# The last tile of a decoder step's second down product, computed in two token parts

## The chip, the cores and the metric

One NeuronCore of a Trainium2 chip runs the whole program. The metric is the device time of one execution in microseconds, as the median of several. Beside it stands one execution taken by the hardware profiler, from which all rows below come.

## What is computed

One inference step of a one-layer decoder. 528 prompt tokens (16 learned meta tokens and 512 of the prompt) and 32 sample tokens (8 sequences of 4) pass through the same weights, D = 1024, feed-forward width 2816, everything in float32:

```python
x = x + 0.5 * swiglu(rmsnorm(x, ffn1_norm), ...)
h = rmsnorm(x, mix_norm)          # mLSTM branch and differential attention, gates, output projection
x = x + merged @ w_out
x = x + 0.5 * swiglu(rmsnorm(x, ffn2_norm), ffn2_w_gate, ffn2_w_up, ffn2_w_down)
y_prompt = rmsnorm(xp[:, N_META:], final_norm)
y_sample = rmsnorm(xs, final_norm)
# rmsnorm(x, g): x * rsqrt(mean(x*x over the 1024 channels) + EPS) * g
```

The meta tokens are dropped from `y_prompt`. New keys, values and states are outputs too; they are stored in the middle of the program and the change does not touch them.

## The kernel before

Activations lie channel by partition: `X` is 128 x 8 x 560, eight tiles (`DT`) of 128 channels, and the 560 columns (`T`) are the tokens: 16 meta, 512 prompt, 32 sample. The second feed-forward block leaves the meta tokens out (`c0 = NMETA`), so its products run over 544 tokens, as two halves of 272.

**Products.** Each float32 product is three float32r matmuls: high part of the weights times high and low part of the activations, and low part of the weights times the high part (L391 to L405). `down2` has eight output tiles (L810 to L814). One tile takes two weight panels, s = 0 and 1, of 11 blocks each (`KD`), in the buffers `raw[s]`, `w_hi[s]`, `w_lo[s]`. SyncE loads a panel (L365), ScalarE makes its high part (L370), VectorE its low part (L374). Per panel the order is half, block, term: 66 matmuls of 272 columns, so 132 for a tile. Even tiles go to PSUM banks 0 and 1, odd ones to 2 and 3.

**After each down2 tile i.** VectorE multiplies the PSUM by `rh` (half the reciprocal root of the second norm, L1925) and adds it to `X` (L1927). ScalarE writes `xg`, X times the final gain (L1859), and `sq`, the squares of X (L1860, L1464). VectorE adds the squares to the running sum `acc` (L1901). TensorE transposes `xg` one tile late (`back_y(i-1)`, L825 to L833) in five pieces of 112 tokens into banks 4 to 7, and VectorE copies them to `ytok` (L2477), whose rows are tokens: row tile t holds tokens 112 t to 112 t + 111, meta tokens included.

**After the last tile (i = 7).** `down_last` (L835 to L846) lets TensorE transpose tile 6, then tile 7, then sum `acc` over the channels by five products of a 128 x 112 piece with a column of ones, into bank 4. ScalarE makes the reciprocal root of the mean, `r5`, by Ln (L1864) and Exp (L1866). ScalarE scales row tiles 1 and 3 (L1870), VectorE 0, 2 and 4 (L2489). SyncE stores each row tile when it is scaled, in the order of t, row tile 4 in two pieces (prompt, sample), six stores in all (L766 to L774), and waits for all stores (L775).

What sets the order: every engine has its instruction stream written out by hand, and semaphores are waited on by count. `mm_done[s]` says a panel's product is done, `evac[e]` a bank pair is free, `x_ready` X is updated, `sq_ready` squares are there, `acc_done` the running sum, `xg_ready`, `yt_full`, `yt_done` the gain copy, its transposes, its row copy; `y5_full`, `y5_log`, `y5_ready` the steps of the root; `y_act`, `y_dve` scaled row tiles.

Of the kernel before, what the change touches and what calls it, by code (L numbers as in the profile page):

```python
# [20 lines left out]
D = 1024  # L21
SEQ, NMETA, NB, DSEQ = 512, 16, 8, 4
# [9 lines left out]
T = NP_ + NS  # L32
H2 = T // 2
DT = D // 128
FT = DFF // 128
KD = FT // 2
# [12 lines left out]
G_FFN1, G_MIX, G_FFN2, G_FINAL, G_CW, G_CB, G_ML, G_SUB, G_N = 0, 8, 16, 24, 32, 64, 72, 80, 81  # L49
# [9 lines left out]
C_EPS = C_M1 + 1  # L59
# [58 lines left out]
def build(nc, ins, outs, const_ap):  # L118
    f32, f32r, i32 = mybir.dt.float32, mybir.dt.float32r, mybir.dt.int32
    ACT = mybir.ActivationFunctionType  # L120
    ALU = mybir.AluOpType
# [5 lines left out]
    with ctx:  # L127
# [31 lines left out]
        h_hi = at("h_hi", [128, FT, T], f32r, R)  # L159
        h_lo = at("h_lo", [128, FT, T], f32r, R + FT * T * 4)  # L160

        xtok = at("xtok", [112, 5, D], f32, R)
        ytok = at("ytok", [112, 5, D], f32, xn0)
        xg = at("xg", [128, 2, T], f32, xn0 + 5 * D * 4)
        vecs = at("vecs", [G_N, 128], f32, R + 5 * D * 4)
        lrow = at("lrow", [1, 4, DHD], f32, R + 5 * D * 4 + 512)
# [15 lines left out]
        small2 = at("small2", [128, 448], f32, RW + 5 * T * 4)  # L182
# [82 lines left out]
        ps = ctx.enter_context(nc.psum_tensor("ps", [128, 8, 512], f32))  # L265
# [15 lines left out]
        wlast = wrow.rearrange("p (b t) -> p b t", t=DSEQ)[:, :, DSEQ - 1]  # L281
        wbc = small2[:, 80:208].rearrange("p (h s) -> p h s", h=HM)
        dec8 = small2[0:NB, 208:212]
        r5 = small2[0:112, 400:405]
        r0 = small2[0:112, 408:418]
        srm = small2[:, 320:336].rearrange("p (b k m) -> p b k m", b=2, k=4)
        SAs = small2[:, 336:400].rearrange("p (b m c) -> p b m c", b=2, m=2)
# [215 lines left out]
        def wide(bank, rows_, cols):  # L503

            return ps[0:rows_, bank:bank + 2, :].rearrange("p b n -> p (b n)")[:, 0:cols]
# [79 lines left out]
                 8: ((0, (4,)), (1, (0, 1)), (0, (5,)), (1, (2, 3)), (0, (6, 7)), (1, (4, 5)))}  # L585
        IDLE = {0: 12, 2: 4, 4: 5}
        HI0 = (0, DT, 3 * DT + 1)
        GAIN = (G_FFN1, G_MIX, G_FFN2, G_FINAL)
        block = ctx.enter_context(nc.Block())

# [2 lines left out]
        def _(sp):  # L593
# [169 lines left out]
            stream(p_wo)  # L763
            stream(up2)
            stream(down2)
            for t in (0, 1, 2, 3, 4):  # L766
                sp.wait_ge(y_act if t % 2 else y_dve, t // 2 + 1)
                if t == 0:
                    sp.dma_start(y_prompt[0, 0:96, :], ytok[16:112, 0, :]).then_inc(stored, 16)
                elif t < 4:  # L770
                    sp.dma_start(y_prompt[0, 112 * t - 16:112 * t + 96, :], ytok[:, t, :]).then_inc(stored, 16)
                else:
                    sp.dma_start(y_prompt[0, 432:512, :], ytok[0:80, 4, :]).then_inc(stored, 16)
                    sp.dma_start(y_sample.rearrange("b t d -> (b t) d"), ytok[80:112, 4, :]).then_inc(stored, 16)  # L774
            sp.wait_ge(stored, 16 * (5 + 6 + 6))  # L775


        @block.tensor
        def _(pe):
            def transpose(out, in_, k):  # L780
                return pe.transpose(out, in_, con[0:k, C_ID:C_ID + k])  # L781
# [28 lines left out]
            def down_tile(p, u, j, e, tiles=None):  # L810
                at_ = None if tiles is None else lambda k: u.lo0 + k + 1
                pe.wait_ge(evac[e], j + p.ev0)
                product(pe, p, j * 2 + e, 0, 2 * e, h_hi, h_lo, 0, True, False, tiles=tiles, tile_at=at_)
                product(pe, p, j * 2 + e, 1, 2 * e, h_hi, h_lo, KD, False, True, tiles=tiles, tile_at=at_)  # L814

            def down(p, u):
# [5 lines left out]
                        down_tile(p, u, j, e)  # L822
                loop(pe, p, body, 2, first=1)

            def back_y(i):  # L825

                pe.wait_ge(xg_ready, i + 1)
                if i >= 2:
                    pe.wait_ge(yt_done, i - 1)
                for t in range(5):  # L830
                    mm = transpose(ps[0:112, 4 + 2 * (i % 2) + t // 4, 128 * (t % 4):128 * (t % 4) + 128],
                                   xg[:, i % 2, 112 * t:112 * t + 112], 128)
                mm.then_inc(yt_full, 1)  # L833

            def down_last(p, u):  # L835
                for j in range(p.n // 2):
                    for e in range(2):
                        down_tile(p, u, j, e, tiles=tile_lo if j == 0 and e == 0 else None)
                        if 2 * j + e >= 1:
                            back_y(2 * j + e - 1)  # L840
                back_y(DT - 1)
                pe.wait_ge(acc_done, 3 * (DT - 1))
                pe.wait_ge(yt_done, DT - 1)
                for t in range(5):
                    mm = pe.matmul(ps[0:112, 4, t:t + 1], acc[:, 112 * t:112 * t + 112], ones[:, 0:1], start=True, stop=True)
                mm.then_inc(y5_full, 1)  # L846

            def pair(p, xs_, first=0):
                def body(j, _q, _jn):
# [602 lines left out]
        def _(act):  # L1452
            def copy(out, in_, scale=1.0):
                return act.activation(out, in_, ACT.Copy, scale=scale)
# [396 lines left out]
            rms(2, up2)  # L1851
            gated(up2, ACT.Silu, h_hi)

            def last_tile(i):

                act.wait_ge(x_ready, DT + i + 1)
                if i >= 2:
                    act.wait_ge(yt_full, i - 1)
                copy(xg[:, i % 2, :], X[:, i, :], scale=gcol[:, G_FINAL + i:G_FINAL + i + 1]).then_inc(xg_ready, 1)  # L1859
                square(3, i)  # L1860

            down(down2, last_tile)
            act.wait_ge(y5_full, 1)
            act.activation(r5, ps[0:112, 4, 0:5], ACT.Ln, bias=con[0:112, C_EPS:C_EPS + 1], scale=1.0 / D).then_inc(y5_log, 1)  # L1864
            act.wait_ge(y5_log, 1)
            act.activation(r5, r5, ACT.Exp, scale=-0.5).then_inc(y5_ready, 1)  # L1866
            act.wait_ge(yt_done, DT)
            act.wait_ge(y5_ready, 1)
            for t in (1, 3):
                copy(ytok[:, t, :], ytok[:, t, :], scale=r5[:, t:t + 1]).then_inc(y_act, 1)  # L1870


        @block.vector
        def _(v):
# [46 lines left out]
            def down(p, r, each):  # L1921
                def add(j, e):
                    i = 2 * j + e
                    v.wait_ge(mm_done[1], i + p.before + 1)
                    v.tensor_tensor(tok(t2[e], p), two(2 * e, p), tok(rh, p), ALU.mult).then_inc(evac[e], 1)  # L1925
                    v.wait_ge(evac[e], j + p.ev0 + 1)
                    v.tensor_tensor(X[:, i, p.c0:], X[:, i, p.c0:], t2[e][:, p.c0:], ALU.add).then_inc(x_ready, 1)  # L1927
                    each(i)

                for j in range(p.n // 2):  # L1930
                    for s in range(2):
                        split_lo(v, p, j * 2 + 1, s)
                    add(j, 0)
                    if j < p.n // 2 - 1:
                        for s in range(2):
                            split_lo(v, p, j * 2 + 2, s)
                        add(j, 1)
                    else:
                        prepare(p.next, 0, 0)
                        add(j, 1)  # L1940
                        prepare(p.next, 0, 1)
# [533 lines left out]
            def rows_y(i):  # L2475
                v.wait_ge(yt_full, i + 1)
                v.tensor_copy(ytok[:, :, 128 * i:128 * i + 128],  # L2477
                              wide(4 + 2 * (i % 2), 112, 640).rearrange("p (t n) -> p t n", n=128)).then_inc(yt_done, 1)

            def last_tile(i):  # L2480
                squares(3, i)
                if i >= 1:
                    rows_y(i - 1)
            down(down2, 3, last_tile)
            rows_y(DT - 1)
            v.wait_ge(yt_done, DT)
            v.wait_ge(y5_ready, 1)
            for t in (0, 2, 4):
                v.tensor_scalar(ytok[:, t, :], ytok[:, t, :], r5[:, t:t + 1], None, ALU.mult).then_inc(y_dve, 1)  # L2489


        @block.gpsimd
# [36 lines left out]
```

## Time and profile before

| | us |
|---|---|
| median of 3 executions | 1712.9 (1712.69 to 1718.42) |
| the profiled execution | 1710.33 |
| its span, first to last instruction | 1708.5 |
| TensorE busy in the span | 1655.7 (97%) |
| VectorE, ScalarE busy | 765.4 (45%), 554.6 (32%) |
| chain that ended last: TensorE, ScalarE, VectorE, DMA | 88%, 3%, 3%, 3% |
| last product of down2 ends | at 1689.53 |
| first store of y issued | at 1698.43 |

The span is shorter than the time by 1.8 us, which lie outside the first and last instruction. Starts are microseconds from the span's start. Matmuls are pipelined, so a single matmul's duration is longer than its distance to the next; the pace of a stream is read from starts, or from a chain's stretch divided by its count. "Granted clock" is the share of TensorE's full clock that the chip allowed, 1.0 for 2.4 GHz and 0.5 for 1.2 GHz.

### The profile page before, as it was taken

What the parts mean: (1) busy time and instruction counts of PE and PEld (TensorE: products, weight loads), DVE (VectorE), ACT (ScalarE), POOL (GpSimd) and SP (SyncE); (2) the same over time, 40 slices, a digit from 0 to 9 for tenths busy, and PEclk for the clock granted to TensorE, in tenths of its full rate; (3) what the DMA queues carried; (4) which work ended last, traced back from release to release, by engine and by line L of the source; (5) the groups of instructions that cost most, each with busy time, mean ns of one, the idle gap of its engine ahead of it and who ended that gap; (6) DMA issues with size and microseconds to landing.
All of it is one profiled execution on the core that took longest, in us unless ns stands there. A gap on an engine that the chain in (4) does not pass through costs nothing.

```text
span 1708.5 us, 30634 instructions
## 1 busy us (share of the span) xinstructions
PE 1655.7 (97%) x12836; PEld 1568.2 (92%) x12836; DVE 765.4 (45%) x1150; ACT 554.6 (32%) x845; POOL 4.2 (0%) x20
## 2 busy tenths in 40 slices
PE   7999999999999889999999999989999999999996
PEld 7999999999988667999999977679999999999996
DVE  4333333333682443553337678664453333333332
ACT  5222222222333432542111257562233222222222
POOL 0000000000000000000000000000000000000000
PEclk9999999999999999999999999999999999999998
DMA  5222223222322740233333240643322222223221
GB/s 139 77 86 86 86 86 98 88 85 76 77 75 56 242 153 1 74 87 86 100 92 98 72 183 26 203 145 97 86 87 87 86 86 86 86 86 102 86 85 53
DMA packets 253836, 161.77 MB, mean 95 GB/s; under 512 B 8234, under 2 KB 246047, under 8 KB 253762
## 3 DMA queue, kind: packets, MB, share of 16 engines
q1 hardware_dynamic: 253616, 160.67, 32.3%
q8 instruction: 55, 0.90, 0.2%
q14 instruction: 19, 0.16, 0.0%
q10 hardware_dynamic: 146, 0.04, 0.0%
HBM read 143.14 MB, written 16.40 MB: 93 GB/s over the span
## 4 chain that ended last, share of the span: by engine, by line
PE 88%; ACT 3%; DVE 3%; DMA 3%; issue 1%; SPq 1%; ACTq 0%; DVEq 0%
PE ps L402 73%; PE ps L781 2%; PE ps L969 2%; PE ps L933 1%; PE ps L1257 1%; PE ps L1185 1%; PE ps L1128 1%; PE ps L1301 1%; PE ps L1018 1%; DMA Cb<-in_state_C 1%; DVE small L2329 1%; PE ps L1113 1%; PE ps L1182 1%; PE ps L1260 1%; DMA raw<-in_w_in 0%
## 5 line engine op out<-in xcount | busy, mean ns | idle before, releaser
L402 PE MATMUL ps<-xn_hi,w_hi 128*128 128x272 f32 (+1 forms) x2192 | 635.7, 290 | 5.6 <-DVE w_lo L374 3.4
L402 PE MATMUL ps<-xn_hi,w_lo 128*128 128x272 f32 (+1 forms) x2192 | 637.5, 291 | 0.0
L402 PE MATMUL ps<-xn_lo,w_hi 128*128 128x272 f32 (+1 forms) x2192 | 634.5, 289 | 0.0
L370 ACT ACTIVATE w_hi<-raw 128x1024 fp32r<-128x1024 f32 (+1 forms) x200 | 222.2, 1111 | 823.4 <-PE ps L402 819.6
L402 PEld LDWEIGHTS ps<-xn_hi,w_hi 128*128 128x128 f32 x2192 | 413.6, 189 | 7.2 <-DVE w_lo L374 4.0
L402 PEld LDWEIGHTS ps<-xn_hi,w_lo 128*128 128x128 f32 x2192 | 413.5, 189 | 0.0
L402 PEld LDWEIGHTS ps<-xn_lo,w_hi 128*128 128x128 f32 x2192 | 412.5, 188 | 0.0
L374 DVE TENSOR_TENSOR w_lo<-raw,w_hi 128x1024 fp32r<-128x1024 f32 (+1 forms) x200 | 257.6, 1288 | 214.0 <-ACT w_hi L370 213.6
L402 PE MATMUL ps<-h_lo,w_hi 128*128 128x280 f32 (+1 forms) x704 | 204.7, 291 | 0.0
L402 PE MATMUL ps<-h_hi,w_hi 128*128 128x280 f32 (+1 forms) x704 | 204.7, 291 | 0.0
L402 PE MATMUL ps<-h_hi,w_lo 128*128 128x280 f32 (+1 forms) x704 | 204.6, 291 | 0.0
L402 PEld LDWEIGHTS ps<-h_lo,w_hi 128*128 128x128 f32 x704 | 132.7, 189 | 0.0
L402 PEld LDWEIGHTS ps<-h_hi,w_lo 128*128 128x128 f32 x704 | 132.7, 188 | 0.0
L402 PEld LDWEIGHTS ps<-h_hi,w_hi 128*128 128x128 f32 x704 | 132.6, 188 | 0.0
L1914 DVE TENSOR_TENSOR tB<-ps,tA 128x560 f32<-128x560 f32 (+1 forms) x44 | 32.3, 733 | 160.9 <-PE ps L402 160.9
L1909 DVE TENSOR_TENSOR tA<-ps,rn 128x560 f32<-128x560 f32 (+1 forms) x44 | 32.2, 733 | 132.5 <-PE ps L402 132.5
L1491 ACT ACTIVATE tA<-tA 128x544 f32<-128x544 f32 (+1 forms) x60 | 38.8, 646 | 0.0
L402 PE MATMUL ps<-m_hi,w_hi 128*128 128x272 f32 x128 | 36.9, 288 | 0.8 <-DVE m_lo L2458 0.8
L402 PE MATMUL ps<-o_hi,w_hi 128*128 128x272 f32 x128 | 37.1, 290 | 0.0
L402 PE MATMUL ps<-o_hi,w_lo 128*128 128x272 f32 x128 | 37.0, 289 | 0.0
L402 PE MATMUL ps<-hm_hi,w_lo 128*128 128x272 f32 x128 | 37.0, 289 | 0.0
L402 PE MATMUL ps<-o_lo,w_hi 128*128 128x272 f32 x128 | 36.9, 288 | 0.0
(372 smaller groups left out, 2026.8 us busy)
## 6 DMA issues: line engine op xcount, KB each, us to landing
raw<-in_w_in SPq DMA_DIRECT2D x56, 512.0 KB, 3.8
raw<-in_ffn_w_gate SPq DMA_DIRECT2D x44, 512.0 KB, 3.8
raw<-in_ffn_w_up SPq DMA_DIRECT2D x44, 512.0 KB, 3.8
raw<-in_ffn_w_down SPq DMA_DIRECT2D x32, 704.0 KB, 4.5
Cb<-in_state_C SPq DMA_DIRECT2D x32, 256.0 KB, 4.1
out<-Cb SPq DMA_DIRECT2D x32, 256.0 KB, 3.0
pages<-in_cache_k SPq DMA_DIRECT2D x16, 512.0 KB, 4.7
pages<-in_cache_v SPq DMA_DIRECT2D x16, 512.0 KB, 4.9
```

The costliest lines, as they stand in the source:

```text
L370: act.activation(w_hi[s][:, 0:p.nk, :], raw[s][:, 0:p.nk, :], ACT.Copy).then_inc(hi_done[s], 1)
L374: v.tensor_tensor(w_lo[s][:, 0:p.nk, :], raw[s][:, 0:p.nk, :], w_hi[s][:, 0:p.nk, :].bitcast(f32), ALU.subtract).then_inc(lo_done[s], 1)
L402: mm = pe.matmul(ps[:, bank + half, 0:p.half], w[s][:, k, :], x[:, k0 + k, cols], start=first and k == 0 and a == 0, stop=last and k == p. ...
L781: return pe.transpose(out, in_, con[0:k, C_ID:C_ID + k])
L933: mm = pe.matmul(ps[0:(128, 128, 128, 128, TAIL, 128)[blk], ring_bank(n) + h // 2, DHM * (h % 2):DHM * (h % 2) + DHM], x, mlw[:, 0, i, :], ...
L969: mm = pe.matmul(ps[:, ring_bank(n) + half, 0:H2], mlw[:, 1 if kind == "k" else 2, 2 * h + k, 128 * m:128 * m + 128], cc[:, 2 * h + k, hal ...
L1018: mm = pe.matmul(ps[:, 6, DHM:2 * DHM], vtok[:, blk, DHM * h + 128 * vt:DHM * h + 128 * vt + 128], ktok[:, blk, DHM * h:DHM * h + DHM], st ...
L1113: mm = pe.matmul(ps[:, half, 0:H2], con[0:HM, C_SEL + 128 * h:C_SEL + 128 * h + 128], rows[:, row, half * H2:(half + 1) * H2], start=True, ...
L1128: mm = pe.matmul(out, km[:, 2 * h + k, t0:t0 + nt], qm[:, 2 * h + k, q0:q0 + nq], start=k == 0, stop=k == 1)
L1491: act.activation(tA[:, p.c0:], tA[:, p.c0:], func).then_inc(evac[0], 1)
L1909: v.tensor_tensor(tok(tA, p), two(0, p), tok(rn, p), ALU.mult).then_inc(g_in, 1)
L1914: v.tensor_tensor(tok(tB, p), two(2, p), tok(tA, p), ALU.mult).then_inc(evac[1], 1)
```

## The change

The last tile of `down2` is computed in two parts of tokens, both panels each: part 0 has tokens 16 to 271 (256 columns, bank 2), part 1 tokens 272 to 559 (288 columns, bank 3). Row tiles now have 128 tokens and start behind the meta tokens (`YROWS`: 16, 144, 272, 400, and 432 for the last, which overlaps tile 3 and of which only the 32 sample rows are used). Part 0 has row tiles 0 and 1, part 1 has 2, 3 and 4.

TensorE: `back_y(6)` comes between the parts. In part 1, after its 21st matmul (s = 0, k = 6), comes part 0's block `last_rows(0)`: column sums into bank 0, of `acc` (up to tile 6) and of tile 7's squares, accumulated by TensorE, then two transposes. `last_rows(1)` follows the last product. ScalarE and VectorE have a part 0 and a part 1 of evacuation, add, squares (now ahead of the gain copy), Ln, Exp and row scaling; tile 7's squares are no longer added to `acc` by VectorE. ScalarE has one more Ln of a single element between its parts. Stores: row tiles 0, 1, 2 and the sample rows by SyncE, row tile 3 by ScalarE's queue. Five stores of 512, 512, 512, 512 and 128 KB.

```diff
+        YROWS = [NMETA + 128 * t for t in range(4)] + [T - 128]
+        LAST = ((NMETA, 256, (0, 1)), (NMETA + 256, 288, (2, 3, 4)))
...
-            for t in (0, 1, 2, 3, 4):
-                sp.wait_ge(y_act if t % 2 else y_dve, t // 2 + 1)
...
+            for t, ready in ((0, (y_dve, 1)), (1, (y_act, 1)), (2, (y_dve, 2))):
+                sp.wait_ge(*ready)
+                sp.dma_start(y_prompt[0, 128 * t:128 * t + 128, :], ytok[:, t, :]).then_inc(stored, 16)
+            sp.wait_ge(y_dve, 3)
+            sp.dma_start(y_sample.rearrange("b t d -> (b t) d"), ytok[96:128, 4, :]).then_inc(stored, 16)
...
+            def last_rows(part):
+
+                pe.wait_ge(acc_done, 3 * (DT - 1) - 1)
+                pe.wait_ge(evac[0], down2.ev0 + DT // 2)
+                pe.wait_ge(sq_ready, 3 * DT + part)
+                for t in LAST[part][2]:
+                    for i, squares in enumerate((acc, sq)):
+                        mm = pe.matmul(ps[:, 0, t:t + 1], squares[:, YROWS[t]:YROWS[t] + 128], ones[:, 0:1],
+                                       start=i == 0, stop=i == 1)
+                mm.then_inc(y5_full, 1)
+                pe.wait_ge(xg_ready, DT + part)
+                pe.wait_ge(yt_done, DT - 2)
+                back_rows(DT - 1, LAST[part][2])
+
+            def last_down(p):
+
+                pe.wait_ge(evac[1], p.ev0 + DT // 2 - 1)
+                for part, (c0, n, _) in enumerate(LAST):
+                    for s in range(2):
+                        pe.wait_ge(lo_done[s], p.before + DT)
+                        for k in range(KD):
+                            for a, (w, x) in enumerate(((w_hi, h_hi), (w_hi, h_lo), (w_lo, h_hi))):
+                                mm = pe.matmul(ps[:, 2 + part, 0:n], w[s][:, k, :], x[:, s * KD + k, c0:c0 + n],
+                                               start=s == 0 and k == 0 and a == 0,
+                                               stop=s == 1 and k == KD - 1 and a == 2)
+                            if part == 1 and s == 0 and k == 6:
+                                last_rows(0)
+                    mm.then_inc(mm_done[part], 1)
+                    if part == 0:
+                        back_y(DT - 2)
+                last_rows(1)
...
-                back_y(DT - 1)
-                pe.wait_ge(acc_done, 3 * (DT - 1))
-                pe.wait_ge(yt_done, DT - 1)
-                for t in range(5):
-                    mm = pe.matmul(ps[0:112, 4, t:t + 1], acc[:, 112 * t:112 * t + 112], ones[:, 0:1], start=True, stop=True)
...
+            def last_part(part):
+
+                c0, n, rows_ = LAST[part]
+                cols, r = slice(c0, c0 + n), slice(rows_[0], rows_[-1] + 1)
+                act.wait_ge(x_ready, 2 * DT + part)
+                act.wait_ge(acc_done, 3 * (DT - 1) - 1)
+                act.activation(sq[:, cols], X[:, DT - 1, cols], ACT.Square).then_inc(sq_ready, 1)
+                act.wait_ge(yt_full, DT - 2)
+                scaled(DT - 1, cols)
+                act.wait_ge(y5_full, part + 1)
+                act.activation(r5[:, r], ps[:, 0, r], ACT.Ln, bias=con[:, C_EPS:C_EPS + 1], scale=1.0 / D).then_inc(y5_log, 1)
+                act.wait_ge(y5_log, part + 1)
+                act.activation(r5[:, r], r5[:, r], ACT.Exp, scale=-0.5).then_inc(y5_ready, 1)
+                act.wait_ge(y5_ready, part + 1)
+                act.wait_ge(yt_done, DT + part)
+                t = rows_[1]
+                copy(ytok[:, t, :], ytok[:, t, :], scale=r5[:, t:t + 1]).then_inc(y_act, 1)
...
+                if i == DT - 1:
+                    last_part(0)
+                    act.activation(small[0:1, 60:61], con[0:1, 0:1], ACT.Ln)
+                    last_part(1)
+                    act.wait_ge(y_act, 2)
+                    act.dma_start(y_prompt[0, 384:512, :], ytok[:, 3, :]).then_inc(stored, 16)
+                    return
...
+            def last_parts():
+
+                for part, (c0, n, rows_) in enumerate(LAST):
+                    o, x = tB[:, c0:c0 + n], X[:, DT - 1, c0:c0 + n]
+                    v.wait_ge(mm_done[part], down2.before + DT)
+                    v.tensor_tensor(o, ps[:, 2 + part, 0:n], rh[:, c0:c0 + n], ALU.mult).then_inc(evac[1], 1)
+                    v.wait_ge(evac[1], down2.ev0 + DT // 2 + part)
+                    v.tensor_tensor(x, x, o, ALU.add).then_inc(x_ready, 1)
+                    if part == 0:
+                        rows_y(DT - 2)
+                    t0, nt = rows_[0], len(rows_)
+                    v.wait_ge(yt_full, DT + part)
+                    v.tensor_copy(ytok[:, t0:t0 + nt, 128 * (DT - 1):D],
+                                  wide(6, 128, 640)[:, 128 * t0:128 * (t0 + nt)].rearrange("p (t n) -> p t n", n=128)
+                                  ).then_inc(yt_done, 1)
+                    v.wait_ge(y5_ready, part + 1)
+                    v.wait_ge(yt_done, DT + part)
+                    v.tensor_scalar(ytok[:, t0, :], ytok[:, t0, :], r5[:, t0:t0 + 1], None, ALU.mult).then_inc(y_dve, 1)
+                v.tensor_scalar(ytok[96:128, 4, :], ytok[96:128, 4, :], r5[96:128, 4:5], None, ALU.mult).then_inc(y_dve, 1)
```

## Rows read from the trace of the kernel before

**Rows 1.** The page's head and its first part: busy us, share, instructions.
```profile
span 1708.5 us, 30634 instructions
PE 1655.7 (97%) x12836; PEld 1568.2 (92%) x12836; DVE 765.4 (45%) x1150; ACT 554.6 (32%) x845; POOL 4.2 (0%) x20
```

**Rows 2.** The chain that ended last, its end: start, us, what.
```profile
1672.33 0.55 PE ps L781 x5
1672.88 16.65 PE ps L402 x132
...
1689.55 0.74 DVE tB L1925
...
1690.31 0.74 DVE X L1927
...
1691.07 0.76 ACT xg L1454
1691.83 0.57 ACT sq L1464
...
1692.42 0.74 DVE acc L1901
1693.16 0.75 DVE ytok L2477
...
1694.05 1.69 PE ps L845 x10
...
1695.76 0.27 ACT small L1864
...
1696.04 1.28 ACT L1866
...
1697.34 0.22 ACT small L1866
...
1697.64 1.15 ACT ytok L1454
```

**Rows 3.** Timeline of VectorE in the first down product (280 columns): start, us.
```profile
369.46 0.73 DVE L1925 TENSOR_TENSOR tB<-ps,rh 128x560 f32<-128x560 f32 x1
...
386.51 0.73 DVE L1925 TENSOR_TENSOR tA<-ps,rh 128x560 f32<-128x560 f32 x1
```

**Rows 4.** Timeline of TensorE, narrow float32 passes and 128-column transposes.
```profile
1083.99 0.42 PEld L781 LDWEIGHTS ps<-con,pages 128*128 128x128 f32 x4 [0.60 <-ACT KT L1454]
...
1085.35 1.16 PE L1361 MATMUL ps<-small,Psm 128*128 128x16 f32 x11
```

**Rows 5.** Groups by form: count, busy us, mean ns.
```profile
L2015 DVE TENSOR_TENSOR E<-ps,rn 128x280 f32<-128x280 f32 x8 | 3.5, 441 | 0.0
...
L1828 ACT ACTIVATE ofac<-qkv 128x256 f32<-128x256 f32 x1 | 0.4, 404 | 0.0
```

**Rows 6.** VectorE's timeline of tile 6, and windows behind the products (PEclk).
```profile
1678.26 0.74 DVE L1901 TENSOR_TENSOR acc<-acc,sq 128x560 f32<-128x560 f32 x1 [1.39 <-ACT sq L1464]
...
1694.00:1694.45 0.45, 0.41 (x4) 0.44 (x5) 0.45 (x1) 0.00 (x0) 0.00 (x0) 0.95 0.00 0
1694.45:1695.00 0.55, 0.55 (x5) 0.55 (x5) 0.18 (x1) 0.00 (x0) 0.00 (x0) 0.50 0.00 0
```

**Rows 7.** Timeline of SyncE's queue: start, us.
```profile
1002.02 5.27 SPq L737 DMA_DIRECT2D out<-vtok  x6
...
1658.44 0.37 SPq L365 DMA_DIRECT2D raw<-in_ffn_w_down  x1
1698.43 0.36 SPq L769 DMA_DIRECT2D out<-ytok  x1
1698.85 3.24 SPq L771 DMA_DIRECT2D out<-ytok  x3
```

**Rows 8.** Windows over stores (last: DMA share, GB/s); an issue's KB, us to landing.
```profile
1003.50:1007.50 4.00, 3.26 (x28) 1.21 (x18) 3.77 (x11) 2.08 (x8) 0.00 (x0) 1.00 1.01 413
1699.50:1705.50 6.00, 0.00 (x0) 0.00 (x0) 0.23 (x1) 0.33 (x1) 0.00 (x0) 0.50 0.99 296
...
out<-kout SPq DMA_DIRECT2D x4, 512.0 KB, 2.6
```

More of the change, by code:

```diff
@@ L162, in build @@
         xtok = at("xtok", [112, 5, D], f32, R)
-        ytok = at("ytok", [112, 5, D], f32, xn0)
+        ytok = at("ytok", [128, 5, D], f32, xn0)
         xg = at("xg", [128, 2, T], f32, xn0 + 5 * D * 4)
@@ L283, in build @@
         dec8 = small2[0:NB, 208:212]
-        r5 = small2[0:112, 400:405]
+        r5 = small2[:, 400:405]
         r0 = small2[0:112, 408:418]
@@ L765, in _ @@
             stream(down2)
-            for t in (0, 1, 2, 3, 4):
-                sp.wait_ge(y_act if t % 2 else y_dve, t // 2 + 1)
[L768 to L775, printed above, removed]
+            for t, ready in ((0, (y_dve, 1)), (1, (y_act, 1)), (2, (y_dve, 2))):
[3 more added lines that the diff above has]
+            sp.dma_start(y_sample.rearrange("b t d -> (b t) d"), ytok[96:128, 4, :]).then_inc(stored, 16)
+            sp.wait_ge(stored, 16 * (5 + 6 + 5))
         @block.tensor
@@ L823, in down, with back_rows @@
                 loop(pe, p, body, 2, first=1)
+            def back_rows(i, rows_):
+                for t in rows_:
+                    mm = transpose(ps[:, 4 + 2 * (i % 2) + t // 4, 128 * (t % 4):128 * (t % 4) + 128],
+                                   xg[:, i % 2, YROWS[t]:YROWS[t] + 128], 128)
+                mm.then_inc(yt_full, 1)
             def back_y(i):
@@ L829, in back_y @@
                     pe.wait_ge(yt_done, i - 1)
-                for t in range(5):
-                    mm = transpose(ps[0:112, 4 + 2 * (i % 2) + t // 4, 128 * (t % 4):128 * (t % 4) + 128],
-                                   xg[:, i % 2, 112 * t:112 * t + 112], 128)
-                mm.then_inc(yt_full, 1)
-            def down_last(p, u):
[L836 to L840, printed above, removed]
-                back_y(DT - 1)
-                pe.wait_ge(acc_done, 3 * (DT - 1))
-                pe.wait_ge(yt_done, DT - 1)
-                for t in range(5):
-                    mm = pe.matmul(ps[0:112, 4, t:t + 1], acc[:, 112 * t:112 * t + 112], ones[:, 0:1], start=True, stop=True)
-                mm.then_inc(y5_full, 1)
+                back_rows(i, range(5))
@@ L848, in pair @@
+            def down_last(p, u):
+                for i in range(DT - 1):
+                    down_tile(p, u, i // 2, i % 2, tiles=tile_lo if i == 0 else None)
+                    if i >= 1:
+                        back_y(i - 1)
+                last_down(p)
             def pair(p, xs_, first=0):
@@ L1852, in _, with scaled @@
             gated(up2, ACT.Silu, h_hi)
-            def last_tile(i):
+            def scaled(i, cols):
+                copy(xg[:, i % 2, cols], X[:, i, cols], scale=gcol[:, G_FINAL + i:G_FINAL + i + 1]).then_inc(xg_ready, 1)
+            def last_part(part):
[14 more added lines that the diff above has]
+                copy(ytok[:, t, :], ytok[:, t, :], scale=r5[:, t:t + 1]).then_inc(y_act, 1)
+            def last_tile(i):
+                if i == DT - 1:
[5 more added lines that the diff above has]
+                    return
                 act.wait_ge(x_ready, DT + i + 1)
@@ L1858, in last_tile @@
                     act.wait_ge(yt_full, i - 1)
-                copy(xg[:, i % 2, :], X[:, i, :], scale=gcol[:, G_FINAL + i:G_FINAL + i + 1]).then_inc(xg_ready, 1)
+                scaled(i, slice(0, T))
                 square(3, i)
             down(down2, last_tile)
[L1863 to L1870, printed above, removed]
         @block.vector
@@ L1937, in down @@
                         add(j, 1)
+                    elif p is down2:
+                        last_parts()
                     else:
@@ L2477, in rows_y @@
                 v.tensor_copy(ytok[:, :, 128 * i:128 * i + 128],
-                              wide(4 + 2 * (i % 2), 112, 640).rearrange("p (t n) -> p t n", n=128)).then_inc(yt_done, 1)
+                              wide(4 + 2 * (i % 2), 128, 640).rearrange("p (t n) -> p t n", n=128)).then_inc(yt_done, 1)
             def last_tile(i):
@@ L2483, in last_tile @@
                     rows_y(i - 1)
-            down(down2, 3, last_tile)
[L2485 to L2489, printed above, removed]
+            def last_parts():
[16 more added lines that the diff above has]
+                v.tensor_scalar(ytok[96:128, 4, :], ytok[96:128, 4, :], r5[96:128, 4:5], None, ALU.mult).then_inc(y_dve, 1)
+            down(down2, 3, last_tile)
         @block.gpsimd
```

## The prediction

> **What bounds the kernel now.** I read the page's first part first: TensorE is busy 97% of the span [rows 1], so between the ends of the program only TensorE's own stream counts. The change touches the last 36 us, so I read the chain of waits there [rows 2]. It has three stretches. Tile 7's products run as one unbroken row of 132 matmuls from 1672.88 to 1689.53. Then a serial tail crosses the engines: evacuation, residual add, gain copy, square, running sum, copy of tile 6's rows, column sums, Ln, a table load, Exp. The first row scale starts at 1697.64, so rstd is there at about 1697.6, 8.1 us after the products. The third stretch is stores: the first is issued at 1698.43 [rows 7] and the span ends at 1708.5, 10.1 us later, with the DMA engines full for most of it [rows 8]. So 19.0 us lie behind the last product, over half of it data movement that could have begun earlier.
>
> **The products.** Splitting 2 x 272 tokens into 256 and 288 keeps the number of matmuls (132) and the number of columns (544 per k and term). Pitch now: 16.65 / 132 = 126.1 ns at 272 columns [rows 2]. In the first down product tiles follow at 386.51 - 369.46 = 17.05 us, 129.2 ns at 280 columns [rows 3]. That is 0.39 ns per column, so I take 119.9 ns for 256 and 132.3 ns for 288; 66 of each give 16.65 us again. If a 256-column matmul went no faster than a 272-column one, this would cost 66 x 6.2 = 0.4 us. Part 0 then ends at 1672.88 + 7.91 = 1680.8.
>
> **What is inserted into the product row.** First, tile 6's five transposes now stand ahead of part 1, where before they hid under the evacuation. No row costs them at exactly this place; five cost 0.55 us in the chain [rows 2], and a 128-column transpose costs 0.42 / 4 = 105 ns [rows 4], so 0.6 us. Second, after 21 matmuls of part 1 (1680.8 + 0.6 + 21 x 0.132 = 1684.2) TensorE does part 0's sums and rows: two row tiles x two sources (the running sum and tile 7's squares) x two passes = 8 passes, then two transposes. The nearest warm row with a full stationary matrix and a narrow moving one is 11 passes in 1.16 us; less the last one's length (0.25) that is 91 ns a pass [rows 4]. The cold one is 10 passes in 1.69 us [rows 2], 169 ns. So 0.7 to 1.35 us for the sums and 0.2 for the transposes; with the edges I take 1.1 us, warm because products stand on both sides (bounds 0.9 and 1.6). The last product therefore ends at 1689.53 + 0.6 + 1.1 = 1691.2.
>
> **Do the inserted waits hold it?** VectorE evacuates and adds part 0 in 0.42 us each (441 ns at 280 columns [rows 5]); ScalarE squares 256 columns in 0.40 us [rows 5]. Squares are there at about 1682.1 and the gain copy at 1682.6, while TensorE asks at 1684.2: 2.1 us of slack, and behind this wait stand 45 products. The running sum it also asks for, up to tile 6, was made at 1678.26 + 0.74 [rows 6]. The rest of part 0 runs beside those 45 products (5.95 us): Ln 0.27, load 1.28, Exp 0.22, scaling a row tile 1.15 on ScalarE, then the added Ln with its load, 1.5. ScalarE is free at about 1685.1 + 1.85 + 1.15 + 1.5 = 1689.6; it is wanted at 1692.1, when part 1's residual is added. VectorE's share (copy of tile 6's rows 0.8, part 0's rows 0.45, one scale 0.78) ends near 1687.7, before 1691.2. Without that cover each would cost its own length; the smallest margin is ScalarE's 2.5 us. Part 0's two stores, 1.05 MB, are issued near 1688 and need 2.5 to 3.5 us [rows 8], so they are gone before the last ones start. Nothing else waits in SP's queue: its last weight load was issued at 1658.44 [rows 7].
>
> The trace has both table loads as 1.28 us, Exp's following Ln at once [rows 2]. The Trainium skill (ScalarE: Activation LUTs, What ACT_TABLE_LOAD costs) charges a switch 2.66 us, because a drain of 1.38 us is added. No row of this tail shows that drain. With it on part 0's two remaining loads ScalarE would be free at 1692.4, 0.3 us late.
>
> **The tail after the last product.** Evacuation and add at 288 columns: 0.44 + 0.44 and two handoffs of 0.02 = 0.92 us, where 1.52 us stood. The square, now ahead of the gain copy: 0.43 (between 0.40 at 256 and 0.66 at 560) + 0.02 = 0.45. The gain copy (0.76), the running sum (0.74), the row copy (0.75) leave the path. The sums now have 12 passes in place of 10, because the squares are added by TensorE: 12 x 91 ns + 0.2 = 1.3 us warm, 2.2 us cold. The granted clock fell from 1.0 to 0.5 (2.4 to 1.2 GHz) at about 1694.4, 4.9 us after the products ended [rows 6]; the new sums run from 1.4 to 2.7 us behind them, so I take them as warm. Ln, load, Exp with handoffs as now: 1.83. Sum: 0.02 + 0.92 + 0.45 + 1.3 + 1.83 = 4.5 us, where 8.1 stood. The added Ln only repeats what holds today, where Ln's load also runs under TensorE's work; Exp's load stays on the path. Transposes and row copy of part 1 lie under Ln and Exp. rstd is there at 1691.2 + 4.5 = 1695.7, 1.9 us earlier than now. The scale of 1024 columns up to the issue stays 0.8 us: first late store at 1696.6.
>
> **The stores.** Now six of 2.23 MB in total follow that point; then three of 1.18 MB (512, 512 and 128 KB). Rows of the DMA engines: 2.23 MB of 112-row tiles moved at 296 GB/s while the engines were 99% busy, yet the 512 KB stores of 128 rows of values (`vtok`, issued from 1002.0 on [rows 7]) moved at 413 GB/s, equally busy, and one such store alone lands 2.6 us after its issue [rows 8]. The new stores have the shape of the latter. Around the movement lie 0.6 us ahead of it and 1.6 us behind it (10.07 less 2.23 MB at about 282 GB/s over all of it, 7.9 us). New tail: 0.6 + 1.18 / 0.413 = 2.85 + 1.6 = 5.05 us; at 282 GB/s it is 6.4. The ScalarE store is ready 0.35 us and the sample rows 0.8 us behind the first, both inside its 1.3 us of movement, so neither adds. I take the fast rate, since shape and size match. The Trainium skill (DMA: Bandwidth & Descriptors, The descriptor swizzle) says that with 128 partitions each DMA engine writes one port's partitions; this trace's 413 against 296 GB/s agrees in direction.
>
> **Sum.** Span: 1696.6 + 5.05 = 1701.7, 6.8 us less than 1708.5. The profiled execution took 1710.33 us, 1.8 outside its span, so 1703.5 us. The median shown, 1712.9, is 2.6 above the profiled one; I carry that over: **1706.1 us**, 0.4% less.
>
> **Rivals.**
> *Forecast, stores at 413 GB/s, everything inserted hidden but 1.7 us*: gain 6.8. Chance 0.55.
> *The rate stays at 282 to 296 GB/s*, because the late state of the chip and not the row count sets it: tail 6.4, gain 5.4. For it: the 112-row stores are the only ones at the end of the program, with the other engines idle. Against: equal busy share at unequal bytes. Chance 0.2.
> *Sums and inserted block at cold prices* (169 ns a pass): 0.5 + 0.9 more, gain 5.4, and 3.6 with a 256-column floor as well; with slow stores too 2.2. For it: narrow matmuls are the only work there. Against: the granted clock was full 4.9 us on. Chance 0.13.
> *A larger gain*: Exp's load falls off the path, 1.28 more: 8.1 us. The Trainium skill (ScalarE: Activation LUTs, Table sets) names a set with both ln and exp. Against: this trace reloads between them, and so will the same two calls. Chance 0.08.
> *Slower than before*: TensorE stands in the block inside part 1, with 45 products behind it. Each us costs a us, so it decides from 6.8 us of standing; if it stands so long that the clock falls, as 4.9 us after the products in [rows 6], the 45 products take 169 / 91 of their time, 5.95 x 0.86 = 5.1 more, and the total is 4.9 + 5.1 - 6.8 = 3.2 us slower, 1716.1. It needs part 0's chain to take 7 us instead of the 1.8 worked out. Chance 0.04.
> The change does what it says: the stores of part 0 wait only for work that lies before 1688.
>
> **Range and chances.** Gains from 2.2 to 8.1 carry over 0.9 of the chance; executions shown spread from 1710.3 to 1718.4 about 1712.9, which adds some 2.5 us either way. Low: 1712.9 - 8.1 - 2.8 = 1702.0; high: 1712.9 - 2.2 + 1.8 = 1712.5. A measurement of this kernel can tell 0.5% from no change, 8.6 us. The forecast needs 1.8 us more for that: 0.08 from the larger gain, in part, and some of the forecast's own upper end, together 0.15. Slower by 8.6 us wants the last rival and more: 0.03. Within 0.5%: 0.82.
>
> **What the changed profile would show.** Two runs of 66 matmuls of 256 and 288 columns with pitch 120 and 132 ns; the inserted block 1.7 us in all; last product at 1691.2; sums at full granted clock; rstd 4.5 us behind; three late stores at about 400 GB/s; span 1701.7. Wrong would be an idle TensorE inside part 1, sums at clock 0.5, or stores at 296 GB/s.

## The result and the profile after

| | before | after |
|---|---|---|
| median of 6 executions each, us | 1714.9 | 1706.8 |
| ratio, estimated over all executions (the two medians alone give 0.9953) | | 0.9948, 95% interval 0.9931 to 0.9965 |
| ratio measured again, beside other executions of before | | 0.9959, 0.9945 to 0.9973 |
| profiled execution, us | 1710.33 | 1707.02 |
| its span, us | 1708.5 | 1705.2 |
| first product of tile 7 starts, us | 1672.88 | 1676.04 |
| from there to the end of the span, us | 35.62 | **29.16** |

The median of 1706.8 us lies 0.7 us above the forecast of 1706.1. The last line is the one to reason with. Nearly everything ahead of tile 7 is the same work in both kernels (only the transposes of `xg` and their copies to `ytok` have 128 rows for 112), and it took 3.2 us longer in this execution (why, further below). The stretch that was changed is 6.46 us shorter, where 6.8 was forecast; 6.46 of 1710.3 us is a ratio of 0.9962, inside both intervals.

The chain of waits of the kernel after, its end (start, us, what); the lines answer to [rows 2]. L860 are the products, L780 the transposes, L845 the column sums:

```profile
1675.49 0.55 PE ps L780 x5
1676.04 7.82 PE ps L860 x66
1683.85 0.55 PE ps L780 x5
1684.39 2.79 PE ps L860 x21
1687.18 0.79 PE ps L845 x8
1687.97 0.28 PE ps L780 x2
1688.25 6.00 PE ps L860 x45
...
1694.27 0.47 DVE tB L2542
...
1694.76 0.47 DVE X L2544
...
1695.25 0.45 ACT sq L1893
...
1695.84 1.48 PE ps L845 x12
...
1697.35 0.26 ACT small L1897
...
1698.92 0.21 ACT small L1899
...
1699.16 0.75 DVE ytok L2554
```

The reader is to see that TensorE's row is still unbroken: no "issue" stands between its pieces, so nothing inserted made it wait. The row is now 18.21 us long (16.65 before). From its end at 1694.25 to the end of the last Exp at 1699.13 are 4.88 us; in [rows 2] it was 1689.53 to 1697.56, 8.03 us. From there to the end of the span are 6.07 us, where 10.94 stood. So 1.56 given, 3.15 and 4.87 gained: 6.46.

What covers part 0's work, from ScalarE's timeline of the kernel after:

```profile
1688.29 1.28 ACT L1899 ACT_TABLE_LOAD   x1
...
1689.82 1.15 ACT L1483 ACTIVATE ytok<-ytok,small 128x1024 f32<-128x1024 f32 x1
1690.99 1.28 ACT L1909 ACT_TABLE_LOAD   x1
1692.28 0.20 ACT L1909 ACTIVATE small<-con 1x1 f32<-1x1 f32 x1
1695.25 0.44 ACT L1893 ACTIVATE sq<-X 128x288 f32<-128x288 f32 x1 [2.77 <-DVE X L2544]
```

ScalarE has 2.77 us to spare before part 1's squares, 2.5 by the forecast. The windows of the kernel after (length; busy us and count of TensorE, its weight loads, VectorE, ScalarE, GpSimd; granted clock, DMA share, GB/s):

```profile
1692.00:1693.00 1.00, 1.00 (x10) 1.00 (x8) 0.00 (x0) 0.47 (x2) 0.00 (x0) 1.00 0.99 401
...
1697.00:1697.40 0.40, 0.40 (x5) 0.40 (x5) 0.00 (x0) 0.05 (x1) 0.00 (x0) 1.00 0.00 0
1697.40:1698.00 0.60, 0.42 (x3) 0.06 (x1) 0.14 (x1) 0.58 (x2) 0.00 (x0) 0.53 0.00 0
...
1701.00:1702.00 1.00, 0.00 (x0) 0.00 (x0) 0.00 (x0) 0.00 (x0) 0.00 (x0) 0.50 1.03 414
1702.00:1704.00 2.00, 0.00 (x0) 0.00 (x0) 0.00 (x0) 0.00 (x0) 0.00 (x0) 0.50 0.97 315
```

The first line is part 0's stores beside the products: 401 GB/s, TensorE still full. The next two show the granted clock falling from 2.4 to 1.2 GHz at about 1697.4, 3.2 us after the last product and as the sums ended. The last two are the late stores, and the last of all has the sample rows' small store in it.

### The profile page after: what moved, and what is told of

Read it like the earlier page. It is cut to its first block, busy times and chain, and to the rows that moved or that the text cites. A ratio compares the mean times of both kernels' runs of the same rounds, so it can differ in the third digit from the quotient of the medians.

```text
span 1705.2 us, 30666 instructions
## 1 busy us (share of the span) xinstructions
PE 1659.1 (97%) x12846; PEld 1571.0 (92%) x12846; DVE 765.4 (45%) x1152; ACT 558.1 (33%) x852; POOL 4.2 (0%) x20
## 4 chain that ended last, share of the span: by engine, by line
PE 89%; ACT 3%; DVE 3%; DMA 2%; issue 1%; SPq 1%; ACTq 0%; DVEq 0%
PE ps L402 72%; PE ps L780 3%; PE ps L998 2%; PE ps L962 1%; PE ps L1286 1%; PE ps L1157 1%; PE ps L1214 1%; PE ps L860 1%; PE ps L1047 1%; PE ps L1330 1%; DMA Cb<-in_state_C 1%; DVE small L2381 1%; PE ps L1142 1%; PE ps L1211 1%; DMA raw<-in_w_in 1%
## 5 line engine op out<-in xcount | busy, mean ns | idle before, releaser
L402 PE MATMUL ps<-h_lo,w_hi 128*128 128x280 f32 (+1 forms) x660 | 191.9, 291 | 0.0
L402 PE MATMUL ps<-h_hi,w_lo 128*128 128x280 f32 (+1 forms) x660 | 191.9, 291 | 0.0
L402 PE MATMUL ps<-h_hi,w_hi 128*128 128x280 f32 (+1 forms) x660 | 191.8, 291 | 0.0
L402 PEld LDWEIGHTS ps<-h_lo,w_hi 128*128 128x128 f32 x660 | 124.4, 189 | 0.0
L402 PEld LDWEIGHTS ps<-h_hi,w_lo 128*128 128x128 f32 x660 | 124.3, 188 | 0.0
L402 PEld LDWEIGHTS ps<-h_hi,w_hi 128*128 128x128 f32 x660 | 124.3, 188 | 0.0
L402 PE MATMUL ps<-hm_lo,w_hi 128*128 128x272 f32 x128 | 36.9, 288 | 0.0
```

What stands on the lines that cost most here:

```text
L402: mm = pe.matmul(ps[:, bank + half, 0:p.half], w[s][:, k, :], x[:, k0 + k, cols], start=first and k == 0 and a == 0, stop=last and k == p. ...
```

## The experiments

All are compared by the time from tile 7's first product to the end of the span ("the stage"), read from each kernel's trace. Before 35.62 us, after 29.16 us; a second trace of the changed kernel gave 1703.5 - 1674.35 = 29.15, so tenths mean something here, which they do not in whole times.

### Stores: shape, and when they start

**Row tiles of 128 tokens alone**, in the kernel before:

```diff
-                                   xg[:, i % 2, 112 * t:112 * t + 112], 128)
+                                   xg[:, i % 2, YROWS[t]:YROWS[t] + 128], 128)
...
+                if t < 4:
+                    sp.dma_start(y_prompt[0, 128 * t:128 * t + 128, :], ytok[:, t, :]).then_inc(stored, 16)
```

> The kernel before with one part of the change alone: the row tiles of y hold 128 tokens behind the meta tokens, stored as four stores of 512 KB and one of 128 KB, all at the end, by SyncE. Nothing else moves. From the first store's issue to the end of the span the kernel before took 10.1 us, with 296 GB/s while the DMA engines were full. Theory A (112-row tiles are slow because of their shape): the same 2.23 MB move at about 410 GB/s in 5.4 us, so 7.6 us behind the first issue. Theory B (stores at the program's end are slow whatever their shape): 296 GB/s and 10 us. From tile 7's first product to the end of the span: A 33.2 us, B 35.6 us (before 35.6).

Stage 1709.5 - 1676.86 = 32.64 us. A window of its late stores:

```profile
1703.00:1708.00 5.00, 0.00 (x0) 0.00 (x0) 0.28 (x1) 0.37 (x1) 0.00 (x0) 0.50 1.02 404
```

404 GB/s against the 296 of [rows 8], at the same place in the program and as full a set of DMA engines. From the last Exp's end to the end: 8.39 us, 2.55 less than before. The other 0.43 us of the stage is the sums: ten passes took 1.26 us here and 1.69 in [rows 2], where the clock fell earlier. Theory A holds: the cut of the row tiles sets the rate, not the place in the program. The edit changes the row count, the first row of a tile, and the number and size of the stores (six to five) together, so which of these does it is not separated. One thing speaks for the row count: when the 32-row store of the samples moves at the very end, the rate falls here too, to 262 GB/s from 1708.0 to 1708.5, with the engines as full (share 1.02).

**Early stores held back**, in the kernel after:

```diff
+            sp.wait_ge(y_act, 1)
-            for t, ready in ((0, (y_dve, 1)), (1, (y_act, 1)), (2, (y_dve, 2))):
+            for t, ready in ((0, (y_dve, 2)), (1, (y_dve, 2)), (2, (y_dve, 2))):
```

> The changed kernel with its stores of row tiles 0 and 1 held back until row tile 2 is scaled, so that all five stores stand at the end. If early stores are worth what their bytes take (1.05 MB at 0.41 MB/us = 2.5 us), the span behind tile 7's first product grows from 29.2 to 31.7 us. A rival: the last stores are bound by their landing and not by bytes, then under 1 us more.

Stage 1706.8 - 1675.26 = 31.54 us, 2.38 more. The early stores are worth what their bytes take. Shape and early start together, 2.55 + 2.36 (8.43 us behind the last Exp, less 6.07) = 4.91, are the 4.87 us gained behind the last Exp to within 0.04.

This run also bears on the next question. Two windows of it, and the queues' packets, MB and share of the engines over both together (q1 is SyncE's queue, q10 ScalarE's):

```profile
1701.00:1702.00 1.00, 0.00 (x0) 0.00 (x0) 0.00 (x0) 0.00 (x0) 0.00 (x0) 0.50 1.00 397
1702.00:1703.00 1.00, 0.00 (x0) 0.00 (x0) 0.00 (x0) 0.00 (x0) 0.00 (x0) 0.50 1.02 401
...
q10 hardware_dynamic: 144, 0.52, 66.9%
q1 hardware_dynamic: 83, 0.27, 34.2%
```

Both queues moved 128-row stores in these 2 us, and the rate stayed at about 400 GB/s.

**Late stores on one queue**, in the kernel after:

```diff
+            sp.wait_ge(y_act, 2)
+            sp.dma_start(y_prompt[0, 384:512, :], ytok[:, 3, :]).then_inc(stored, 16)
...
-                    act.dma_start(y_prompt[0, 384:512, :], ytok[:, 3, :]).then_inc(stored, 16)
```

> The changed kernel with row tile 3's store issued by SyncE behind row tile 2's, not by ScalarE. In the changed kernel the rate fell from 414 to 315 GB/s when ScalarE's store joined. Theory A (two queues in flight share the engines badly): over 400 GB/s throughout and about 0.5 us less. Theory B (the sample rows' small store or the tail end of the movement does it): same rate, and the end within 0.2 us of 29.2 us behind tile 7's first product.

Stage 1705.7 - 1676.85 = 28.85 us, 0.31 less. Two windows of its late stores:

```profile
1702.00:1704.00 2.00, 0.00 (x0) 0.00 (x0) 0.00 (x0) 0.00 (x0) 0.00 (x0) 0.50 1.01 401
...
1704.00:1705.00 1.00, 0.00 (x0) 0.00 (x0) 0.00 (x0) 0.00 (x0) 0.00 (x0) 0.50 0.75 201
```

The first looks like 401 GB/s in place of 315, but it is not the same stretch of the stores: the last Exp of this run ended at 1699.95, 0.82 us later than in the kernel after. The window that answers to 1702 to 1704 there is 1702.8 to 1704.8 here, with 338 GB/s, and its last part has the 32-row store (268 GB/s from 1704.0 to 1704.75, engines full). So neither theory holds as written. Theory A expected over 400 GB/s throughout and 0.5 us; the held-back stores above moved at 400 GB/s from two queues, and behind the last Exp they took 8.43 us where the row tiles of 128 tokens alone, all from one queue, took 8.39. Theory B had the small store right, since the rate falls with one queue too, but not the end, which came 0.31 us earlier. What the runs show is narrower: with row tile 3's store and the small one moving at the same time from two queues, the DMA engines were busy 3.3 us for the late bytes; one behind the other from one queue, 3.2 us. The queue and the order of these two stores changed together, and which of them costs is open.

The Trainium skill (DMA: Bandwidth & Descriptors, Issuing engines are not separate DMA queues) says that issuing from several engines only saves issue time; here that saving was smaller than what else the second queue changed.

### The tail behind the products

**Tile 7's squares summed by TensorE, alone**, in the kernel before, one part, 112-row tiles:

```diff
-                pe.wait_ge(acc_done, 3 * (DT - 1))
-                pe.wait_ge(yt_done, DT - 1)
+                pe.wait_ge(acc_done, 3 * (DT - 1) - 1)
+                pe.wait_ge(sq_ready, 3 * DT)
...
+                    for i, squares in enumerate((acc, sq)):
```

> The kernel before with one part of the change alone: tile 7's squares are made ahead of the gain copy and summed over channels by TensorE beside the running sum (20 passes in place of 10, 112-column pieces), tile 7's transposes behind the sums. One part, 112-row tiles and stores as before. Expected from the last product to the last Exp's end: 0.02 + 1.52 + 0.67 + 0.15 + 20 x 0.123 + 1.82 = 6.6 us, where it was 8.05 us: 1.4 us less, 34.2 us behind tile 7's first product. Rival: the row copies on VectorE then end last and nothing is won.

From the last product (1691.64) to the last Exp's end (1697.92) 6.28 us, 1.75 less than before: this part of the idea works by itself, and better than the 6.6 expected (20 passes took 2.11 us, not 2.46). The stage is 1709.9 - 1674.99 = 34.91 us, only 0.7 less, because the stores, which the edit did not touch, took 1.04 us longer (295 GB/s, and a long issue of the last one):

```profile
1702.46 1.19 SPq L773 DMA_DIRECT2D out<-ytok  x1
1703.70 2.76 SPq L774 DMA_DIRECT2D out<-ytok  x1
```

Why that issue took 2.76 us was not tried. None of the kernels with 128-row tiles showed it.

**The running sum's passes first**, in the one-queue kernel:

```diff
-                pe.wait_ge(sq_ready, 3 * DT + part)
-                for t in LAST[part][2]:
-                    for i, squares in enumerate((acc, sq)):
+                for i, squares in enumerate((acc, sq)):
+                    if i == 1:
+                        pe.wait_ge(sq_ready, 3 * DT + part)
+                    for n, t in enumerate(LAST[part][2]):
```

> The changed kernel with all late stores on SyncE's queue, and in each part's sums the passes over the running sum ahead of the wait for tile 7's squares (each row tile's sum in a bank of its own), so that in part 1 six of twelve passes run while TensorE waits. Expected behind the one-queue kernel's 28.85 us: 6 x 0.123 = 0.74 us less, 28.1 us. If the time of the sums is the entering and leaving and not the passes, under 0.3 us less.

Stage 1705.4 - 1677.28 = 28.12 us, 0.73 less than with one queue, where 0.74 was expected. Its chain shows six passes behind the squares where twelve stood:

```profile
1696.50 0.45 ACT sq L1899
...
1696.99 0.84 PE ps L851 x6
```

**Sqrt and reciprocal for Ln and Exp**, on top of that (the added Ln goes too):

```diff
-                act.activation(r5[:, r], ps[:, 0:len(rows_), part], ACT.Ln, bias=con[:, C_EPS:C_EPS + 1], scale=1.0 / D).then_inc(y5_log, 1)
-                act.wait_ge(y5_log, part + 1)
-                act.activation(r5[:, r], r5[:, r], ACT.Exp, scale=-0.5).then_inc(y5_ready, 1)
+                act.activation(r5[:, r], ps[:, 0:len(rows_), part], ACT.Sqrt, bias=con[:, C_EPS:C_EPS + 1], scale=1.0 / D).then_inc(y5_log, 1)
...
+                    v.reciprocal(r5[:, t0:t0 + nt], r5[:, t0:t0 + nt]).then_inc(y5_ready, 1)
```

> As the kernel with the running sum's passes first, and Ln, table load, Exp replaced by one Sqrt on ScalarE (its table loaded ahead) and a reciprocal on VectorE. Ln to Exp took 1.82 us; Sqrt 0.29, reciprocal 0.17 and the row copy of 0.56, which then stands on the path, make 1.07: 0.75 us less, 27.35 us behind tile 7's first product. If Sqrt's table is loaded on the path after all, 1.3 us more than that.

Stage 1700.2 - 1672.89 = 27.31 us. From the end of the sums to the scale 1693.45 to 1694.53, 1.08 us, with the row copy in it:

```profile
1693.47 0.27 ACT small L1903
...
1693.77 0.18 DVE small L2550
1693.95 0.48 DVE ytok L2552
...
1694.53 0.75 DVE ytok L2557
```

ScalarE loads a table once in this tail, at 1682.50 in part 0, and not again. The kernel was then timed:

> The kernel with Sqrt, running sum first and one queue, timed. Its stage behind tile 7's first product took 27.3 us where the kernel before took 35.6: 8.3 us of about 1713, so a ratio of 0.9951 to the kernel before, and about 1.8 us less than the changed kernel. If the ratio of the changed kernel (0.9948, 8.9 us) were all the tail's doing, this one should be near 0.994.

Ratio 0.9957 (0.9941 to 0.9972), median 1704.3 us. Its stage was 27.30 us again. The changed kernel, timed beside it:

> The changed kernel again, timed beside the same runs of the kernel before. The stage behind tile 7's first product was 6.5 us shorter: a ratio of 0.9962. The first measurement gave 0.9948 (0.9931 to 0.9965). If the stage is the whole of it, this one comes nearer 0.996.

Ratio 0.9959 (0.9945 to 0.9973), median 1704.9 us. So by stage the Sqrt kernel beats both others, by 1.85 and 8.3 us; whole times cannot tell it from the changed kernel.

**Without the added Ln:**

```diff
-                    act.activation(small[0:1, 60:61], con[0:1, 0:1], ACT.Ln)
```

> The changed kernel without the added Ln of one element between ScalarE's parts. Part 1's Ln then needs its table behind the gain copy, from 1.9 us after the last product to 3.2 us after it; the sums end 3.1 us after it. So 0.1 us more, 29.2 us behind tile 7's first product, as the cover of TensorE's sums hides the load. If the load waits for the sums, 1.3 us more.

Stage 1707.4 - 1678.16 = 29.24 us, 0.08 more. The added instruction buys next to nothing, since the sums hide the load but for the last 0.1 us: it ended at 1699.54, and the sums, at the kernel after's distance from the squares, at about 1699.44.

### Covers and rivals

**Part 0's block 42 matmuls later:**

```diff
-                            if part == 1 and s == 0 and k == 6:
+                            if part == 1 and s == 1 and k == 9:
```

> The changed kernel with part 0's sums and transposes put after the 63rd matmul of part 1, not after the 21st, 5.6 us later. This tests the cover that the prediction claimed for ScalarE and VectorE. If the margins were real, ScalarE (free 2.75 us before part 1's residual is added) now ends its part 0 and the extra Ln 2.8 us after that moment, VectorE 1.9 us after the last product: 2.8 us more, 32.0 us from tile 7's first product to the end of the span (29.2 in the changed kernel). If those chains never limit, 29.2 us. No idle TensorE inside part 1 either way.

Stage 1710.5 - 1677.38 = 33.12 us, 3.96 more, not 2.8. ScalarE's squares did start 2.73 us later in the stage, as worked out. The rest is this:

```profile
1698.90:1699.89 0.99, 0.00 (x1) 0.04 (x1) 0.00 (x0) 0.98 (x4) 0.00 (x0) 0.52 1.01 406
1699.89:1702.59 2.70, 2.70 (x13) 2.70 (x14) 0.00 (x0) 0.28 (x1) 0.00 (x0) 0.50 0.40 159
```

TensorE stood for 4.3 us waiting for the squares, the granted clock was at 1.2 GHz when it began, and twelve passes took 2.70 us where the changed kernel's took 1.48. That is 1.22 us more, and 2.73 + 1.22 = 3.95. The cover is real, and a wait that uses it up costs more than its own length.

**Parts of 384 and 160 tokens:**

```diff
-        LAST = ((NMETA, 256, (0, 1)), (NMETA + 256, 288, (2, 3, 4)))
+        LAST = ((NMETA, 384, (0, 1, 2)), (NMETA + 384, 160, (3, 4)))
```

> The changed kernel with the parts cut 384 and 160 tokens: row tiles 0, 1, 2 in part 0, row tile 3 and the sample rows in part 1 (row tile 3 stored by SyncE, sample rows scaled and stored by ScalarE). If a matmul's pace stays linear in its columns (0.39 ns each), 160 columns take 82 ns: block 0.5 us longer, tail 0.9 us shorter, late stores 0.66 MB in place of 1.18 MB, 1.3 us shorter; 27.4 us behind tile 7's first product. If a narrow matmul has a floor near 100 ns (the narrow passes' 91 to 99 ns), 66 of them cost 1.2 us more: 28.6 us.

Stage 1706.7 - 1677.15 = 29.55 us, worse than the change. Its chain:

```profile
1677.15 11.57 PE ps L860 x66
...
1689.26 2.31 PE ps L860 x21
...
1693.22 5.00 PE ps L860 x45
```

A matmul of 384 columns took 175 ns, one of 160 columns 111 ns. The changed kernel's 256 and 288 took 118.5 and 133 ns, about 0.46 ns a column, by which 160 would have been 75. So below 256 columns the pace of a float32r matmul with a new 128 x 128 stationary matrix hardly falls any more, 7.5 ns for 96 columns, and 111 ns looks like its floor, higher than either theory had it. (The column sums, one moving column and a new 128 x 128 stationary matrix for every pass, follow each other at 111 ns too, as shown below; widths between 1 and 160 were not tried.) The product row grew by 2.87 us (21.08 against 18.21), and the tail (4.07 against 4.88) and the stores (4.40 against 6.07) gave back 2.5.

### Why the stretch ahead of tile 7 differs

In thirteen traces, all with nearly the same work ahead of it, tile 7 starts between 1672.88 and 1678.16. The first place where the kernels before and after part is the stage of the sample states. The chain of the kernel before there:

```profile
555.83 3.82 DMA nst<-in_state_n
559.70 0.89 PE ps L781 x6
...
561.02 0.44 PE ps L781 x4
```

and of the kernel after:

```profile
555.82 4.75 DMA nst<-in_state_n
560.62 1.35 PE ps L780 x6
...
562.82 0.85 PE ps L780 x4
```

One load of 32 KB landed 0.9 us later, and the four transposes behind it took 0.85 us, not 0.44. The windows of the kernel after say why:

```profile
560.00:562.00 2.00, 1.38 (x7) 1.34 (x8) 0.41 (x2) 0.22 (x1) 0.00 (x0) 0.70 1.02 347
562.00:564.50 2.50, 2.50 (x11) 1.96 (x11) 0.00 (x0) 1.19 (x2) 0.00 (x0) 0.56 0.12 38
```

TensorE stood for the load, its clock was halved, and by 564 us the execution was 2.5 us behind the other, most of the 3.2 us at tile 7. This is a difference between executions and not between kernels: the two traces of the Sqrt kernel, one and the same program, start tile 7 at 1672.89 and 1677.70. Why the load landed later was not tried. It is nearly half the effect under study, and enough to explain why the two measured ratios differ by 0.0011 (1.9 us).

## Why the prediction held, point by point

**The products.** Right: 118.5 and 133.2 ns a matmul (119.9 and 132.3 said), 16.61 us for the 132 in the end, as for 2 x 272. The alternative, no gain below 272 columns, fell at 256; the 160-column run shows that the floor is real but lies lower.

**What is inserted.** 0.55 for tile 6's transposes (0.6 said), 0.79 + 0.28 for the block (1.1 said). At full clock, as argued.

**The waits.** Right. TensorE did not stand in part 1, and the margins of ScalarE (2.8 us, 2.5 said) and VectorE (3.7 us, 3.5 said) were there. Moving the block used both up: VectorE's evacuation of part 1 then started 1.8 us after the last product, ScalarE's squares 2.7 us later in the stage.

**The tail.** 4.88 us from the last product to Exp's end, 4.5 said. The mis-sized term is the sums: 12 passes in 1.48 us and 0.14 ahead of them, 1.62 against 1.3. The 91 ns a pass came from a row that does not have a full stationary matrix throughout, as I had said it does; a third of its weight loads are 32 columns wide. The line of the kernel before says so:

```profile
L1361 PEld LDWEIGHTS ps<-small,Psm x96: 106/192/192, 1085.1 to 1134.0; 128*128 128x128 f32 x64, 128*32 128x32 f32 x32
```

The kernel after's own pairs of passes, from TensorE's timeline, between the products and behind the wait:

```profile
1687.16 0.36 PE L845 MATMUL ps<-ones,sq 128*128 128x1 f32 x2
1687.39 0.36 PE L845 MATMUL ps<-ones,acc 128*128 128x1 f32 x2
...
1696.06 0.36 PE L845 MATMUL ps<-ones,sq 128*128 128x1 f32 x2
1696.28 0.36 PE L845 MATMUL ps<-ones,acc 128*128 128x1 f32 x2
```

In both places pairs start 0.22 us apart, 111 ns a pass. So being alone costs a pass nothing; the 123 ns that 1.48 / 12 gives, and the 140 of the six-pass run, hold the length of the last pair, 0.36 us. Of the 0.32 us that were missed, 0.24 are the pace and 0.08 the edges. That the sums would run at full clock held, but the clock fell as they ended, 3.2 us behind the last product and not 4.9 as in [rows 6]. How near the other case was I had not seen.

**The stores.** 6.07 us from Exp's end, against 0.87 up to the issue and 5.05 behind it, 5.9 in all. The shape argument held: 404 against 296 GB/s at the same place. Its parts were less good than their sum. The 0.6 us ahead of the movement were 0.8 and the 2.85 us of movement were 3.5, since the 128 KB of sample rows do not move at 413 GB/s (262 to 303 GB/s in the half microsecond in which they end the stores of four runs) and ran beside a big store; the 1.6 us behind it were 0.9. Which rows a DMA engine serves, on which the prediction leaned for the direction, no run shows.

**The rivals.** "The rate stays at 296" fell with the first experiment, though 315 GB/s with the small store in flight lay near it. "Cold sums" did not come about, and the late block shows its price: 225 ns a pass. My 169 came from a row whose first 0.4 us ran at full clock ([rows 6]), so it was a mixture. The sum of that rival was wrong as well: a 256-column floor was priced at 0.4 us, so the gain with it is 5.0 and not 3.6, with slow stores 3.6 and not 2.2, and the range's upper end should have been 1711.1. "Exp's load off the path" did not happen by itself; with Sqrt in its place 0.8 us were won, not 1.28, since the row copy then stands there. "Slower than before" had the right mechanism and needed a longer stall than any run had: in the late-block kernel 4.3 us of standing, behind the products and not among them, made it 4.0 us worse than the changed kernel and still 2.5 better than before. A stall inside part 1 was not tried.

**The drain of a table switch.** The 1.38 us that the Trainium skill (ScalarE: Activation LUTs, What ACT_TABLE_LOAD costs) adds to each load is in none of these traces: the instruction behind a load starts 0.01 to 0.02 us after it (1689.57 to 1689.58 in the kernel after), the load itself 0.02 us after the Ln ahead of it, and ScalarE was free 2.8 us early. The measurement decides.

**Size against noise.** By stage the gain is 0.38% of the time, "within 0.5%" as forecast. By whole times it is 0.52% (0.35 to 0.69%) the first time, just beyond, and 0.41% the second, so whole times do not decide on which side of 0.5% it lies.

**Luck.** That the median came within 0.7 us of 1706.1 is mostly luck. The profiled span was 3.5 us above the forecast 1701.7 (3.2 before tile 7, 0.3 in the stage), and the 2.6 us carried over from profiled execution to median were -0.2 this time. The two misses nearly cancel. The starting point was loose too: the kernel before has a median of 1712.9 over the three executions known then and 1714.9 over six. The number to trust is the stage, 6.46 us against 6.8.

## What to carry to other kernels

At the end of a program, split the last piece of compute so that the finished part's stores leave under the rest; what they gain is their bytes over the store rate, as long as each engine's share of the finished part fits under the remaining products with some us to spare. Read that slack engine by engine from the timeline, since a wait that outlasts it can also cost TensorE's clock, as the 4.3 us of standing did here. Give stores all 128 partitions, and do not count on the full rate for a store of few rows or while one runs beside a big one; do not cut a matmul below the width where its pace stops falling; and compare the changed stage in the trace when whole executions differ by as much as the effect.

## What the runs showed of the hardware that was not expected

- Two kinds of tile, equally full DMA engines: the stores of 112-row tiles (with one each of 96, 80 and 32 rows) moved at 295 to 296 GB/s (two kernels), stores of 128 rows at 397 to 414 GB/s, from one queue or from two.
- A store of 32 rows at the end brings the rate down to 262 to 303 GB/s with the engines full (four kernels). Beside a 512 KB store from another queue: 315 GB/s over 2 us, where one behind the other from one queue made 338.
- A float32r matmul with a new stationary matrix takes 111 ns at 160 columns, 118.5 at 256, 126.1 at 272, 133 at 288, 175 at 384.
- Passes of a float32 column sum (one column moving, a new 128 x 128 stationary matrix each) start 111 ns apart at full clock, between products and behind a wait alike, and 212 ns apart at half clock (1699.89 to 1702.01 in the late-block kernel).
- A load that landed 0.9 us later cost 2.5 us by 564 us, as TensorE's clock was halved behind it.
